# A seven-product down projection for six pairs of row tiles, and work made ahead at both ends of the convolution stage

## The reference

```
def swiglu(h, wg, wu, wd):
    return (jax.nn.silu(h @ wg) * (h @ wu)) @ wd
# every layer
x = x + g_m * rmsnorm(y, norm_mix_post)          # y = mixer output @ w_out
h = rmsnorm(x, norm_ffn_pre) * (1 + sc_f) + sh_f
f = swiglu(h, w_ffn_gate, w_ffn_up, w_ffn_down)  # 1024 -> 2816 -> 1024
x = x + g_f * rmsnorm(f, norm_ffn_post)
# mixer of the second layer
a, g, u, v = split(h @ w_in_cd); hist = a * sigmoid(g)   # then a 31-tap convolution
y = concat([yc, yd]) @ w_out_cd
```

## Time and profile before

| | us |
|---|---|
| Median of 3 runs | 2962.05 (2953.34 to 2963.36) |
| Profiled execution | 2957.34 |
| Its span | 2955.6 |
| PE busy, matmuls | 2791.9 in 24,793 instructions |
| DVE, ACT, POOL busy | 1757.3, 1074.0, 1195.7 |
| Mean granted clock | 0.972 |

### The profile page before, as it was taken

The page is one execution under the profiler, slowest core; times in us unless marked ns, Lnnn a source line. Parts: engine busy times, 40 slices in busy tenths (PEclk is TensorE's granted clock), DMA queues, the critical chain, the costliest instruction groups (busy, mean ns, idle before and its releaser), DMA issues. The chain is left out here.

```text
span 2955.6 us, 60037 instructions
## 1 busy us (share of the span) xinstructions
PE 2791.9 (94%) x24793; PEld 2546.5 (86%) x24793; DVE 1757.3 (59%) x3048; ACT 1074.0 (36%) x2145; POOL 1195.7 (40%) x822
## 2 busy tenths in 40 slices
PE   6999999999998989999999998898999999999997
PEld 4887776666668989999999987878988999999997
DVE  5341245588874776666652277976487666664235
ACT  4511026522224643333320045765553333331012
POOL 2411137733315634444432134784544444443111
PEclk7999999999998999999999998999999999999999
DMA  9546400177753312323264233101332322346322
GB/s 301 203 166 216 138 20 4 43 285 272 269 182 96 120 67 89 118 89 103 104 247 169 94 98 112 42 29 44 92 102 82 104 103 95 112 153 233 133 96 87
DMA packets 232394, 377.86 MB, mean 128 GB/s; under 512 B 14522, under 2 KB 155195, under 8 KB 223668
## 3 DMA queue, kind: packets, MB, share of 16 engines
q1 hardware_dynamic: 200108, 253.95, 25.8%
q0 software_dynamic: 11776, 75.50, 7.1%
q10 hardware_dynamic: 20240, 44.57, 4.1%
HBM read 298.71 MB, written 73.28 MB: 126 GB/s over the span
## 5 line engine op out<-in xcount | busy, mean ns | idle before, releaser
L805 PE MATMUL ps<-HS,w_split 128*128 128x272 f32 x1920 | 272.5, 292 | 20.1 <-POOL w_split L1402 9.8
L805 PEld LDWEIGHTS ps<-HS,w_split 128*128 128x128 f32 x1920 | 252.9, 190 | 26.2 <-ACT sg L1067 14.4
L821 PE MATMUL ps<-HS,w_ring 128*128 128x272 f32 x1920 | 273.6, 289 | 0.0
L821 PEld LDWEIGHTS ps<-HS,w_ring 128*128 128x128 f32 x1920 | 254.3, 189 | 0.0
L2370 PEld LDWEIGHTS ps<-HS_in,w_split 128*128 128x128 f32 x1728 | 222.9, 191 | 27.3 <-issue 16.4
L1787 DVE TENSOR_TENSOR Y<-Y,ps 128x272 f32<-128x272 f32 x256 | 112.1, 438 | 224.7 <-PE ps L821 224.7
L2370 PE MATMUL ps<-HS_in,w_split 128*128 128x272 f32 x1728 | 233.9, 294 | 8.7 <-DVE HS_in L2590 8.6
L1402 POOL TENSOR_TENSOR w_split<-w_raw,w_split 128x512 fp32r<-128x512 f32 x120 | 170.4, 1434 | 154.3 <-ACT w_split L1059 154.3
L776 PE MATMUL ps<-HS,w_ring 128*128 128x272 f32 x1344 | 178.8, 294 | 17.7 <-PEq L3508 10.5
L776 PEld LDWEIGHTS ps<-HS,w_ring 128*128 128x128 f32 x1344 | 174.5, 192 | 20.3 <-POOLq L1438 10.7
L1402 POOL TENSOR_TENSOR w_ring<-w_raw,w_ring 128x512 fp32r<-128x512 f32 x40 | 62.6, 1564 | 269.5 <-ACT w_ring L1059 269.5
(11 more groups left out here) (517 smaller groups left out, 6346.2 us busy)
## 6 DMA issues: line engine op xcount, KB each, us to landing
hid_spill<-hid SPq DMA_DIRECT2D x40, 1088.0 KB, 7.4
w_mod_half<-w_mod_in SPq DMA_DIRECT2D x40, 1024.0 KB, 6.4
HS<-hid_spill ACTq DMA_DIRECT2D x32, 1088.0 KB, 10.5
w_raw<-w_ffn_gate_in SPq DMA_DIRECT2D x44, 512.0 KB, 4.2
w_raw<-w_ffn_up_in SPq DMA_DIRECT2D x44, 512.0 KB, 4.3
w_raw<-w_ffn_down_in SPq DMA_DIRECT2D x44, 512.0 KB, 4.6
x_part<-x_spill SPq DMA_DIRECT2D x54, 272.0 KB, 3.1
x_spill<-Y SPq DMA_DIRECT2D x12, 1088.0 KB, 5.7
```

Of the source, the lines that this page charges most:

```text
L805: ins = pe.matmul(psum(U.banks(u)[b]), part_slot(j, a)[:, k, :], token_part(n, j, e)[:, k, :], start=(j < 3 and k == 0 and i == 0), stop=( ...
L821: ins = pe.matmul(down_bank(n), slots[DOWN_SLOT[t]][:, a, d * P:(d + 1) * P], hid_cols(k, t, q)[:, e, :], start=(t == lo and j == 0), stop ...
```

## The change

**Down projection.** Pairs 3 to 8 (`PAIRS`, 12 row tiles) leave the direct form. Chunks are now 2, 2 and, last, 6 row tiles. Between the second and the last come six passes (`NPASS`): pass p treats two pairs (k = p // 2) on one half of the columns (n = p % 2). A pass has seven products (`halved`), each with 4 output banks `d`, 2 tiles and 3 matmuls: 24 matmuls. All 8 banks are used, 4 by even and 4 by odd products. DVE adds two banks at a time (`add_product`) into `Y` and into a shared area (rows 7 of `HS`), and `merge` distributes it at the end.

**Operands of the passes.** Weight side: per pair, two DVE sums (`row_sums`), two POOL differences, seven ACT copies and seven POOL subtractions of 128 by 512 (`row_high`, `row_low`). Token side: the up units of the six pairs store three of their four blocks, and besides four sums of blocks: `hidden_sums` on DVE in place, `sums_high` on ACT and `sums_low` on POOL into `y_r` (free columns of `Y`), then `store_sums` by SP into `part_spill`. ACT's sums of a first up unit stand in the following unit, those of the second up unit after the sigmoids of the following gate unit. They wait until the previous sums are stored. The gate unit two units later waits, in `sigmoid`, until POOL has read the buffers (`sum_lo`).

**Ends of the convolution stage.** `CD_AHEAD` is 6; three sigmoids and one gate product are made in the first tail (`first_gate_ahead`). At the end of `stage_cd` two output units (`out_unit`, q = 0, d = 0 and 1) are made before the barrier, a third weight tile is made ready and a fourth loaded; `low_d(2)` moves from DVE to POOL, `shift(3)` ahead of the last `take_u`.

```diff
-CHUNKS = ((0, 2), (2, 4), (4, 8), (8, 12), (12, 16), (16, 22))
+CHUNKS = ((0, 2), (2, 4), (4, 10))
+PAIRS = tuple(range(3, NFG - 2))
+NPASS = len(PAIRS)
...
+            sp.wait_ge(prod, S0)
             load_hid(sp, 1)
             store_hid(END - 1)
-            for t in range(4, NROWS):
+            load_pair(0)
+            load_pair(1)
...
+            for p in range(3, NPASS):
+                load_pair(p)
+                for h in range(2):
+                    load_tokens(p, h)
+            load_last(sp, 0)
+            for t in range(CHUNKS[NCHUNK][0], NROWS):
                 load_down(t)
+            load_last(sp, 1)
...
+            def halved(p, i):
...
+                for d in range(KH):
...
+                            pe.wait_ge(products_added, 2 * (f - 2) + d // 2 + 1)
...
+                    for u in range(2):
+                        for j, (a, e) in enumerate(((0, 0), (0, 1), (1, 0))):
+                            ins = pe.matmul(psum(product_bank(p, i, d)), row_part(2 * k + u, i, a)[:, d * P:(d + 1) * P],
...
             def sigmoid(u, i):
...
                     if U.held(u):
                         act.wait_ge(hid_lo, U.held(u))
+                        if U.UNIT[u - 2][1] in PAIRS:
+                            act.wait_ge(sum_lo, 4 * U.summed(u - 1))
...
+            def sums_high(u):
+                m, f, mat, n = U.UNIT[u]
+                for x, (i, s) in enumerate(SUM_ORDER):
+                    act.wait_ge(sum_made, 4 * U.summed(u) + x + 1)
+                    if x == 0 and U.summed(u):
+                        act.wait_ge(sum_out, 32 * U.summed(u))
+                    act.activation(sum_high(s), gate_buf(U.gate_of(u), i), ACT.Copy).then_inc(sum_hi, 1)
...
             for m in range(1, NBATCH):
                 for j in range(NPROD):
                     part_low(m, j)
+                if m >= 2 and U.BATCH[m - 1][1] and U.BATCH[m - 1][0] in PAIRS:
+                    for u in (U.FIRST[m - 1], U.LAST[m - 1]):
+                        sums_low(u)
...
+                if mat and f in PAIRS:
+                    for i in (0, 1, 3):
+                        hidden_low(u, i)
+                    hidden_sums(u)
...
                         for i in range(4):
                             hidden_low(U.PAIR0, i)
-                        dve.wait_ge(hid_lo, 8 * NFG)
+                        dve.wait_ge(hid_lo, 8 + U.lows(END))
+                        row_sums(0)
...
-CD_AHEAD = 5
+CD_AHEAD = 6
+CD_BANKS = 5
+CD_GATES, CD_TAKES = 3, 1
+OUT_AHEAD = 2
```

More of the change, by code:

```diff
@@ L685, in store_out @@
                 sp.dma_start(dst, xo[t % 4][0:n, :]).then_inc(o_out[t % 4], 16)
-            for t in range(ready, KD):
+            for t in range(2, KD):
                 early_load(t)
@@ L1149, in half @@
                     part_high(m + 1, 4)
+                if late is not None and n:
+                    sums_high(late)
                 finish(2)
                 finish(3)
+                if late is not None and not n:
+                    sums_high(late)
                 if soon:
@@ L1373, in _ @@
                 samples_high()
+                for q in range(1, 3):
+                    first_gate_ahead(q)
             if out:
@@ L3840, in silu, with shift @@
             def silu(i):
+                sigmoid(i)
+                shift(i)
+            def shift(i):
                 q = CD_ORDER[i]
-                sigmoid(i)
                 for k in range(KA):
@@ L3917, in _ @@
             high_c(1)
+            high_d(2)
             to_hi(len(CD_TILES))
[L3919 to L3920 removed]
+            sigmoid(2)
+            to_hi(len(CD_TILES) + 1)
+            shift(2)
+            sigmoid(3)
             high_c(2)
[L3922 to L3923 removed]
+            to_hi(len(CD_TILES) + 2)
             high_d(3)
@@ L3997, in _ @@
             low_c(1)
-            to_lo(len(CD_TILES))
-            to_lo(len(CD_TILES) + 1)
+            low_d(2)
+            for t in range(3):
+                to_lo(len(CD_TILES) + t)
         @block.vector
```

386 lines of the change are left out of this document (317 added, 69 removed).

## The result

| | before | after |
|---|---|---|
| Median | 2961.36 us (4 runs) | 3071.41 us (3066.53 to 3077.86, 4 runs) |
| Profiled execution, span | 2957.34, 2955.6 | 3066.53, 3064.2 |
| Matmuls | 24,793 | 24,505 |
| Mean granted clock | 0.972 | 0.967 |

The change makes the kernel slower: the ratio is 1.038, with a 95% interval of 1.0366 to 1.0400. The forecast was 2998 us, with a range up to 3035. The direction was right, but the loss is 109 us between the profiled executions (110 between the medians) where 41 were forecast.

A forecast was written before the change was run, and what follows sets the result against it. PE was taken as the bound: its matmul count times pace, plus places where it stands. The terms -36.1 - 3 - 8 + 53 + 12 + 22 + 1 = +41 on 2957.3 gave 2998 us, range 2965 to 3035.

The forecast's parts named there:

- Unit stage: Six pairs of units per tail: two waits and what queues behind them cost 4.4 us a pair, +53 us.
- Hold at product 6: Gate unit: POOL's late subtractions hold the sigmoid, so PE's product 6 waits for add_22, 1.9 us a pair.
- Store chain: Second up unit's sums wait for the first's store, delaying copy_a and the next unit's product 3: about 2 us.
- DVE's seven instructions instead of four: Ahead of the next unit's sums: 1.2 to 1.7 us more on DVE, partly beside PE; 0.5 us taken.
- The paragraph on exclusion: Passes: POOL's eight new subtractions a pair could delay DVE multiplications, 29 us in all; nothing was added.
- Start of the down projection: DVE's two new sums wait for pair 0's raw weights, delaying the 17th bank: 6 us a tail, +12.
- End of the passes: Before the last chunk, PE waits for late weight tiles: 10 us plus 1 for the clock, +22 both tails.
- Within the passes: Inside the six passes: DVE and POOL both have room, +1 us.
- Rival C: The passes are bound by transfers; at 180 GB/s 65 us more, 3063 us; chance 0.07.
- Ends of the convolution stage: Work moved into PE's gaps at the first tail's end (-3 us) and the convolution stage's end (-8 us).
- A: Only the down projection stalls, the units' sums hide: 2950 us; chance 0.15.
- B: Everything hides and the matmul count decides: 2920 us, faster; chance 0.16.

The follow-up runs named there:

- no_dve_sums: The changed kernel without DVE's eight sums of blocks a pair; ACT, POOL and the stores work on the blocks instead: 3057.74 us.
- no_pool_sums: The changed kernel without POOL's subtractions for the sums, except the first unit's; DVE's sums, ACT's copies, stores and waits stay: 3066.52 us.
- sums_on_dve: The changed kernel with POOL's low sums on DVE, sums placed anew, split early stores, copy_a ahead of two weight copies, down projection queues reordered: 2942.06 us.
- down_loads: The changed kernel with SP's loads for the down projection issued earlier and DVE's row_sums(0) and row_sums(1) set later: 3034.07 us.
- no_sums: The changed kernel without the sums of blocks on DVE, ACT and POOL (except the first unit's) and ACT's waits for them; stores remain: 2974.74 us.
- dve_sums_later: The changed kernel with DVE's hidden_sums moved later in its queue, behind multiplications of the following unit: 3073.08 us.

## Why the prediction was wrong

**Matmuls removed (-36.1).** Right: 288 fewer at the same pace. The six passes take 126.8 us for 1008 matmuls, 0.1258 each.

**Unit stage (+53, bounds 18 and 78).** This is the term that was mis-sized, it measured +102.6, and it lies outside its bounds. Two of its steps were far too small, DVE's sums and what follows the store, and the sum was formed as if their costs were independent. Its steps:
- *Hold at product 6 (1.9).* The mechanism was right. It measured 1.27 and 1.28 where DVE's sums are out of the way; in the changed kernel it is hidden by the stall in front of it.
- *Store chain (2.0).* Right in mechanism too, too small: 3.50 and 3.59 in the same two kernels, and 1.2 to 1.4 more on average in the slow products behind it. This alone would have broken the term: in no_dve_sums, where DVE's sums are left out, hold and store come to 7.0 us a pair instead of 3.9, +83.5 for both tails. I counted 7.4 us for the two transfers. In no_dve_sums it was 9.6 from POOL's last subtraction (to 1264.8) to ACT's copy (1274.39), with two weight loads and four hidden stores issued in the 3 us before the store; that these made it longer is argued, not shown.
- *DVE's seven instructions instead of four (0.5, between 0 and 1).* This step failed. I took their own length, 1.7 us, beside PE. The four of the second up unit took 4.7 with POOL's subtractions beside them, and cost 2.70 us at `add_b` of the next gate unit and 1.6 in slow products behind it; those of the first cost 0.66 at `add_b` of the second up unit. They also make `copy_a` late: 1.13 instead of 0.49, and 0.44 in no_dve_sums. Together 5.5 to 6.1 us a pair where PE stands in the changed kernel, instead of 0.5. Taking them away gives back only 1.6, because the other chain stands behind them.
- *The rule that spoke against the change.* The paragraph on exclusion priced only POOL's eight new subtractions, as delays of DVE's multiplications, and set them to nothing because the multiplications stand behind the held sigmoid. It left out DVE's eight new sums, which meet POOL's old weight subtractions. no_pool_sums shows that these are enough for 1.47 and 1.41 us. Being stretched is not enough by itself, though: in sums_on_dve the sums are as long, in other places, and the unit stage is 41 us a tail shorter than in the changed kernel.
- *The upper bound.* I added waits of one chain. With two chains that are late at the same time each one alone costs almost all: 483 us a tail without DVE's part, 489.6 without POOL's, 492.6 with both, 443 with neither. The low clock after the longest stall, which I counted in the down projection only, is another 1.0 to 1.6 us a pair.

**Start of the down projection (+12, bounds 7 and 16).** The place and the cause were right: DVE's 17th bank behind `row_sums(0)`, 7.7 us instead of 5. The load, issued at 1561.28 behind the hidden store, was there at 1568.85: 7.6 us for both halves, where I had 4.6 and 0.6. With the clock it is 10 a tail, from down_loads (58.2 to 48.1), so +20, above the upper bound of 16: the landing time was mis-sized here.

**End of the passes (+22, bounds 14 and 32).** Right: 13.25 us where the count gave 11 and I took 10, and 1.5 of low clock, +29, inside the bounds.

**Within the passes (+1).** Right: 0.6 a tail. Rival C is out, transfers keep up.

**Ends of the convolution stage (-11).** About -3. PE's idle time in the first gap fell by 1.4 us and in the second by 2.6, though three units more are made in the gaps. The second gap was not shortened by two units; what stands there now are waits for the third and the fourth weight tile, the delay that the prediction named as its lower case (0.96 and 2.34 us on POOL, with 3.90 for DVE ahead of the two units). No run takes these edits apart.

**The rivals.** A and B asked for hidden sums. no_sums shows that even without any sums this kernel is 0.4 to 0.8% slower than before, so A's 2950 was too low too: the stalls of the down projection alone take back what the matmuls and the ends give. B, a faster kernel, came up only with the queues in another order and the low parts of the sums on DVE.

## What to carry to other kernels

Where an engine is 60% busy, ask what an added instruction stands in front of, and what runs beside it on an engine that it excludes, not how long it is by itself: four such sums took 1.9 us in dve_sums_later and 4.7 in the changed kernel. Leave out each new part alone and all together before naming a culprit; if the parts do not add up, there are parallel chains, and an edit that shortens one of them shows next to nothing. Loads that the next stage needs belong in the queue ahead of anything that waits for the current stage's end; here that, with DVE's sums of weights set later, gave back 25 us a tail without an instruction more.

## What was not expected of the hardware

Stalls of 2.70 and 3.59 us inside a dense stretch were followed by slow products (2.71 and 1.93 us from start to start instead of 1.50, and 2.88 and 2.52), while after 1.27, 1.33 and 1.92 us the next product was only 0.1 late. So these two stalls cost 4.5 and 6.1 us in all. The length of the one stall does not decide it: in no_pool_sums one of 1.81 us, with one of 1.15 ahead of the product before it (the 2.70 had one of 1.13 there), was followed by products of 2.15 and 2.48 us, 1.6 lost. Giving an engine at 62% the work of one at 44%, with the sums placed anew, made the kernel 2.7% faster (3023.85 to 2942.06 us): DVE does these 272-column subtractions in 0.43 us where POOL needs 0.74 to 0.96. How much of the gain is due to that and how much to the new places, stores and order of ACT no run takes apart.
